# Rotary rows fetched by DMA within SBUF and copied to PSUM by ScalarE, in place of a TensorE product, beside three in-projections

## The reference

```python
def rope(x, pos):
    d = x.shape[-1]
    ...
    x1, x2 = xf[..., :d // 2], xf[..., d // 2:]
    return jnp.concatenate([x1 * cos - x2 * sin, x2 * cos + x1 * sin], axis=-1).astype(x.dtype)
```

## Time and profile before

| | |
|---|---|
| median of three runs | 3206.18 us (3196.72 to 3207.56) |
| profiled execution | 3206.65 us, span 3204.9 us |
| granted TensorE clock, mean | 0.969 of full speed |
| busy TensorE / VectorE / ScalarE / GpSimd | 3026.6 / 1619.9 / 1035.1 / 1096.7 us |
| layer 1's in-projection | about 993 to 1081 us |
| layer 2's | about 1706 to 1882 us |
| layer 3's | about 2438 to 2613 us |

### The profile page before, as it was taken

The page is one execution under the profiler, slowest core; times in us unless marked ns, Lnnn a source line. Parts: engine busy times, 40 slices in busy tenths (PEclk is TensorE's granted clock), DMA queues, the critical chain, the costliest instruction groups (busy, mean ns, idle before and its releaser), DMA issues.

```text
span 3204.9 us, 47400 instructions
## 1 busy us (share of the span) xinstructions
PE 3026.6 (94%) x16972; PEld 2445.0 (76%) x16972; DVE 1619.9 (51%) x2705; ACT 1035.1 (32%) x1842; POOL 1096.7 (34%) x634
## 2 busy tenths in 40 slices
PE   6998899999999898999998998999999999999997
PEld 4766688888877766889886766788877867688886
DVE  3466677753336574524236866442343367642423
ACT  4153421111224364322234334422223236532222
POOL 1262133323223313344442410344445311244443
PEclk8999999999999999999998998999999999999999
DMA  6202144433221002232321210323324100123322
GB/s 258 104 24 79 40 131 144 151 125 125 64 61 47 21 2 73 65 92 91 92 92 56 79 34 4 105 92 98 98 86 119 53 27 1 35 98 93 97 93 84
DMA packets 73202, 258.97 MB, mean 81 GB/s; under 512 B 9328, under 2 KB 11889, under 8 KB 70513
## 3 DMA queue, kind: packets, MB, share of 16 engines
q1 hardware_dynamic: 60256, 205.61, 20.4%
q10 hardware_dynamic: 12816, 51.65, 4.7%
HBM read 253.03 MB, written 2.10 MB: 80 GB/s over the span
## 4 chain that ended last, share of the span: by engine, by line
PE 85%; DVE 5%; issue 4%; ACT 2%; POOL 1%; ACTq 1%; DMA 1%; PEld 1%; POOLq 1%; SPq 1%; DVEq 0%; PEldq 0%
PE ps L852 59%; PE ps L818 7%; PE ps L2725 3%; PE ps L2739 2%; DVE ps L398 1%; PE ps L2893 1%; PE ps L2222 1%; PE ps L435 1%; PE ps L1123 1%; PE ps L2028 1%; PE ps L2955 1%; PE ps L2033 1%; ACT w_hi L638 1%; POOL w_lo L776 1%; PEld ps L852 1%
## 5 line engine op out<-in xcount | busy, mean ns | idle before, releaser
L776 POOL TENSOR_TENSOR w_lo<-w_raw,w_hi 128x1024 fp32r<-128x1024 f32 (+1 forms) x373 | 920.7, 2470 | 1752.9 <-ACT w_hi L638 1613.8
L638 ACT ACTIVATE w_hi<-w_raw 128x1024 fp32r<-128x1024 f32 (+1 forms) x373 | 386.2, 1038 | 1194.8 <-PE ps L852 984.8
L852 PE MATMUL ps<-h_hi,w_hi 128*128 128x258 f32 (+2 forms) x1824 | 327.4, 322 | 28.9 <-ACT w_hi L638 15.4
L852 PEld LDWEIGHTS ps<-h_hi,w_hi 128*128 128x128 f32 x1824 | 269.6, 191 | 64.4 <-ACT w_hi L638 17.3
L852 PE MATMUL ps<-h_lo,w_hi 128*128 128x258 f32 (+2 forms) x1824 | 317.0, 316 | 0.0
L852 PE MATMUL ps<-h_hi,w_lo 128*128 128x258 f32 (+2 forms) x1824 | 316.8, 316 | 0.0
L852 PEld LDWEIGHTS ps<-h_hi,w_lo 128*128 128x128 f32 x1824 | 267.8, 190 | 23.9
L852 PEld LDWEIGHTS ps<-h_lo,w_hi 128*128 128x128 f32 x1824 | 268.3, 190 | 23.3
L940 DVE CAST act_hi<-f_t 128x512 f32 (+1 forms) x88 | 167.5, 1903 | 12.5
L852 PE MATMUL ps<-hb_hi,w_hi 128*128 128x512 f32 x672 | 166.7, 390 | 1.8 <-issue 1.8
L852 PE MATMUL ps<-act_hi,w_hi 128*128 128x512 f32 (+1 forms) x660 | 153.4, 373 | 14.1 <-ACT w_hi L638 13.5
(11 more groups left out here) (357 smaller groups left out, 4940.5 us busy)
## 6 DMA issues: line engine op xcount, KB each, us to landing
w_raw<-in_ffn_in SPq DMA_DIRECT2D x176, 512.0 KB, 3.5
mod_row<-in_w_mod_rows ACTq DMA_DIRECT2D x64, 512.0 KB, 4.4
w_raw<-in_ffn_out SPq DMA_DIRECT2D x64, 512.0 KB, 3.5
w_raw<-in_ev_in SPq DMA_DIRECT2D x26, 512.0 KB, 3.5
w_raw<-in_ffn_out SPq DMA_DIRECT2D x32, 384.0 KB, 3.0
w_raw<-in_od_in SPq DMA_DIRECT2D x21, 512.0 KB, 3.5
mod_ring<-in_w_mod SPq DMA_DIRECT2D x8, 1024.0 KB, 14.3
wide_ring<-in_w_mod_wide ACTq DMA_DIRECT2D x8, 1024.0 KB, 5.0
```

What stands on the lines that cost most here:

```text
L638: act.activation(k.w_hi[:, s, 0:self.KT * P], k.w_raw[:, s, 0:self.KT * P], ACT.Copy).then_inc(k.sems["w_hi_ready"], 1)
L776: ins = pool.tensor_tensor(k.w_lo[:, s, 0:self.KT * P], k.w_raw[:, s, 0:self.KT * P], k.w_hi[:, s, 0:self.KT * P].bitcast(F32), ALU.subtract)
L852: ins = pe.matmul(k.ps[:, self.step * s + g, 0:t1 - t0], w[:, s, c * P:(c + 1) * P], h[:, c, t0:t1], start=(n == 0), stop=(n == len(parts) ...
```

## The change

- TensorE's product of line 1123 is gone for layers 1 to 3 (`tensor` does nothing in `RopeBeside`; layer 0 keeps its own). The minus sign that was in the matrix is now in the first half of each group of the sine table, and the matrix of layer 0 loses its sign likewise.
- SP, after issuing the load of slab m, waits until the tile of slab m - 4 is out and until the copy of the tile two before it has been made, and issues 128 / half transfers of half rows x 2 KB each within SBUF: `swapped` gets the tile with the halves of each group exchanged. `swapped` has two buffers. After the last slab SP does this for four more turns.
- ScalarE, at turn s + 3, waits for these transfers and for the bank (`rot_done`), and copies `swapped` into the bank.
- VectorE's steps of the rotation move one turn later (multiply and add at turn s + 2, low part at s + 3), ScalarE's high part too (s + 4). GpSimd's cosine product stays.
- What builds on the rotated tiles moves one turn later: the index scores, RELUs and sums, the rounds and the selection in layer 2; `FIRST` = 12 in layer 3.

```diff
+            if isinstance(self.beside, RopeBeside):
+                self.beside.sync(sp, m)
 
         self.slabs(sp, load)
+        if isinstance(self.beside, RopeBeside):
+            for m in range(self.M, self.M + RopeBeside.BEHIND):
+                self.beside.sync(sp, m)
...
+    BEHIND = 4
...
-    def tensor(self, pe, m):
-        n = self.at(m - 1)
+    def sync(self, sp, m):
+
+        n = self.at(m - self.BEHIND)
         if n is None:
             return
-        self.is_out(pe, m - 1)
-        if n >= len(self.BANKS):
-            pe.wait_ge(*self.count("rot_done", n - len(self.BANKS) + 1))
-        pe.matmul(self.bank(n), self.tiles[n].get("rot", self.rot), self.src(n), start=True, stop=True).then_inc(self.kit.sems["rot_mm"], 1)
+        self.is_out(sp, m - self.BEHIND)
+        if n >= 2:
+            sp.wait_ge(*self.count("rot_in_psum", n - 1))
+        h = self.tiles[n].get("half", self.half)
+        for p in range(0, P, h):
+            q = p + h if p // h % 2 == 0 else p - h
+            sp.dma_start(self.swapped[p:p + h, n % 2, :], self.src(n)[q:q + h, :]).then_inc(self.kit.sems[f"swapped{n % 2}"], 16)
+
+    def tensor(self, pe, m):
+        pass
...
     def vector(self, dve, chain, m):
         S = self.kit.sems
-        n = self.at(m - 2)
+        n = self.at(m - 3)
...
-        n = self.at(m - 1)
+        n = self.at(m - 2)
         if n is not None:
             tile = self.tiles[n]
-            dve.wait_ge(*self.count("rot_mm", n + 1))
+            dve.wait_ge(*self.count("rot_in_psum", n + 1))
...
     def scalar(self, act, chain, m):
+        n = self.at(m - 4)
+        if n is not None and "lo" in self.tiles[n]:
+            tile = self.tiles[n]
+            act.wait_ge(*self.count("rot_sum", n + 1))
+            if "plain" in tile:
+                act.activation(tile["plain"], self.bank(n), ACT.Copy)
+            if tile["hi"].shape[-1] > SEQ:
+                act.activation(tile["hi"][:, SEQ:], self.linear.tile(m - 4)[:, 0, SEQ:], ACT.Copy)
+            act.activation(tile["hi"][:, 0:SEQ], self.bank(n), ACT.Copy).then_inc(self.kit.sems["rot_hi"], 1)
         n = self.at(m - 3)
...
+        if n is not None:
+            act.wait_ge(self.kit.sems[f"swapped{n % 2}"], self.b_dma[n % 2] + 16 * sum(self.dmas[n % 2][:n // 2 + 1]))
+            if n >= len(self.BANKS):
+                act.wait_ge(*self.count("rot_done", n - len(self.BANKS) + 1))
+            act.activation(self.bank(n), self.swapped[:, n % 2, :], ACT.Copy).then_inc(self.kit.sems["rot_in_psum"], 1)
...
-    SCORES, TURNED, OUT, PAIRS, FIRST = 2, 3, 6, 8, 11
...
+    SCORES, TURNED, OUT, PAIRS, FIRST = 2, 3, 6, 8, 12
...
-            out[p, 0], out[p, 1] = np.cos(ang), np.sin(ang)
+            out[p, 0], out[p, 1] = np.cos(ang), np.sin(ang) * f(-1 if p % group < half else 1)
```

More of the change, by code:

```diff
@@ L1084, with __init__ @@
     BANKS = (4, 5, 6)
-    def __init__(self, kit, linear, rot, table, rot_c, tiles):
-        self.kit, self.linear, self.rot, self.table, self.rot_c = kit, linear, rot, table, rot_c
+    BEHIND = 4
+    def __init__(self, kit, linear, half, table, rot_c, swapped, tiles):
+        self.kit, self.linear, self.half, self.table, self.rot_c, self.swapped = kit, linear, half, table, rot_c, swapped
         self.tiles = tiles
         linear.attach(self)
-        self.b = {name: kit.reserve(name, len(tiles)) for name in ("rot_mm", "rot_cos", "rot_sum", "rot_done")}
+        self.b = {name: kit.reserve(name, len(tiles)) for name in ("rot_in_psum", "rot_cos", "rot_sum", "rot_done")}
         self.b["rot_hi"] = kit.reserve("rot_hi", sum("lo" in tile for tile in tiles))
+        self.b_dma, self.dmas = [], []
+        for e in range(2):
+            self.dmas.append([P // tile.get("half", half) for tile in tiles[e::2]])
+            self.b_dma.append(kit.dma_count(f"swapped{e}", sum(self.dmas[e])))
     def at(self, s):
@@ L1174, with __init__ @@
     AT = 6
-    def __init__(self, kit, linear, rot, table, rot_c, tiles, first_v, v_tok, keys):
-        super().__init__(kit, linear, rot, table, rot_c, tiles)
+    def __init__(self, kit, linear, half, table, rot_c, swapped, tiles, first_v, v_tok, keys):
+        super().__init__(kit, linear, half, table, rot_c, swapped, tiles)
         self.first_v, self.v_tok, self.keys = first_v, v_tok, keys
@@ L1238, with __init__ @@
     GATES, MAIN, SMALL = slice(0, 192), slice(192, 320), slice(320, 384)
-    SCORES, TURNED, OUT, PAIRS, FIRST = 2, 3, 6, 8, 11
-    def __init__(self, kit, linear, rot, table, rot_c, tiles, w1, w1_in, first_v, toks, q0):
-        super().__init__(kit, linear, rot, table, rot_c, tiles)
+    SCORES, TURNED, OUT, PAIRS, FIRST = 2, 3, 6, 8, 12
+    def __init__(self, kit, linear, half, table, rot_c, swapped, tiles, w1, w1_in, first_v, toks, q0):
+        super().__init__(kit, linear, half, table, rot_c, swapped, tiles)
         self.q0 = q0
@@ L1669, with __init__ @@
     PAIRS, ROUNDS, LATENT, NOPE, VALUES = 4 * QT, TOPK // 8, 6, 8, 22
-    def __init__(self, kit, linear, rot, table, rot_c, tiles, loaded, w_uk):
-        super().__init__(kit, linear, rot, table, rot_c, tiles)
+    def __init__(self, kit, linear, half, table, rot_c, swapped, tiles, loaded, w_uk):
+        super().__init__(kit, linear, half, table, rot_c, swapped, tiles)
         self.loaded, self.w_uk = loaded, w_uk
@@ L1747, in scalar @@
             act.dma_start(k.w_uk[:], self.w_uk).then_inc(S["uk_in"], 16)
-        if 6 <= m < 10:
-            for u in range((m - 6) * QT, (m - 5) * QT):
+        if 7 <= m < 11:
+            for u in range((m - 7) * QT, (m - 6) * QT):
                 out, n = self.pair(u)
@@ L1789, in vector @@
             dve.wait_ge(*self.count2("iw_in", 1))
-        if 4 <= m < 8:
-            self.add_scores(dve, chain, m - 4)
-        if m == 8:
+        if 5 <= m < 9:
+            self.add_scores(dve, chain, m - 5)
+        if m == 9:
             dve.wait_ge(*self.count2("idx_acc", self.PAIRS))
@@ L2850, in plan @@
                    [(0, 1, HD ** -0.5), (1, 2, 8 ** -0.5), (2, 7, 1.0), (7, 8, A_SCALE), (8, 18, 1.0), (18, 22, HD ** -0.5), (22, 26, 1.0)], norm=g.pre, tiles=EV_TILES, close=True)
[L2851 to L2852 removed]
+    small_rope = {"half": 16, "table": k.table[:, 1]}
+    LatentBeside(k, ev_in, 32, k.table[:, 0], k.rot_c2, k.swapped2,
                  [{"slab": s} for s in (0, 2, 3, 4, 5)] + [{"slab": s, **small_rope} for s in (7, 12, 13)]
@@ L3083, in rot @@
         for p in range(P):
-            if p % group < half:
-                m[p + half, p] = -1
-            else:
-                m[p - half, p] = 1
+            m[p + half if p % group < half else p - half, p] = 1
         return m
```

29 lines of the change are left out of this document (10 added, 19 removed).

## The result

The changed kernel took 3184.02 us (median of 6, 3182.56 to 3188.13) against 3205.78 us of the kernel before (median of 6): a ratio of 0.9935 with a 95% interval of 0.9925 to 0.9945. In a later series, beside three of the experiments, it took 3186.52 (median of 5) against 3204.43: 0.9948 (0.9935 to 0.9962). The gain is 18 to 22 us; 26.8 were forecast, and the time was forecast as 3180. The first trace has a span of 3184.7 us.

The account below looks back on a forecast made before the run. TensorE, busy for 94% of the span, was taken to bound the kernel. 35.8 us removed less 5.4 (index scores) and 3.6 (VectorE's lag and layer ends) gave 26.8 off 3206.18: 3179.4, say 3180; range 3168 to 3200.

Parts of the forecast that it names:

- Removed, 35.8 us: TensorE, layers 1 to 3: 40 rotations removed, 10 at 0.85 us and 30 at 0.91 us, 35.8 us in all.
- SyncE's period p: Layer 1 to 3 transfers: time per issue 0.43 us, 0.46 with the gap; a layer 1 turn is 0.36 + 8p = 4.0 us.
- the ring: Layer 1, weight split through GpSimd, SP, landing and copy to next split but one: 10.2 of 11.4 us, fits below p = 0.61.
- the queue: SP's turn in layer 1, 0.36 + 8p, binds when it exceeds TensorE's 5.7 us, at p = 0.67.
- rival 1: Layer 1: copies pace it mildly, at p = 0.97 a turn takes 8.1 us; 19 us back, 3199 us; chance 15%.
- 8 x excess: Layer 1: eight slabs each charged the SP turn's excess over 5.7 us, 8 x 2.4 = 19 us at p = 0.97.
- Rival 2: Layer 1: copies pace it fully, p from 1.1 us, and the kernel is slower, 3226 us at p = 1.26; chance 8%.
- (a) Index scores, 5.4 us: Layer 2's score groups: rotation worth 0.38 us there (1.6 lost), copies ahead of RELUs 1.8, late rows 2.0; bounds 1.6 and 10.
- (b) VectorE behind in layer 2, 0.8 us at the end: Layer 2's top-k rounds: DVE falls behind 0.52 us per slab, last selection ends some 0.8 us after today's next-stage start.
- (c) Ends, 1.4 + 1.4 us: Ends of layers 1 and 3: multiply and add ahead of V tile, 2 x 0.7 us; last compressed pair moved, 1.4 us.
- Layer 3, 11.3 us forecast: Layer 3's gain: removed work less the forecast's losses there, 11.3 us.

Follow-up runs that it names:

- 16 transfers: Changed kernel with each layer 1 tile fetched by sixteen transfers of 8 rows instead of eight of 16: 3231.91 us, ratio 1.0083 to the kernel before.
- the RELUs first: Changed kernel with ScalarE's RELUs of layer 2's index scores ahead of its copy of swapped rows: 3178.64 us, ratio 0.9920 to the kernel before.

## Why the forecast held, and where its terms were off

The sign, the size and the range were right (3180 forecast, 3184 and 3187 measured), and so was the shape: TensorE bound the kernel, the removed work counted almost in full in plain slabs, and what was lost was lost at the score groups and the ends. The terms:

- **Removed, 35.8 us.** Right. Free of the clock's part the three layers gained 7.2, 6.9 and 10.4 us, 24.5 together, against a forecast of 26.8 for just that. Slabs start 5.70 us apart in layer 1 and 5.44 in layer 2's plain ones, to the hundredth.
- **SyncE's period p, taken as 0.46 us: too low by a third and more.** It was 0.62 to 0.74 as a mean over eight, with the load 0.58. By the forecast's own test (the ring binds from 0.61, the queue from 0.67) layer 1 was over the limit, and rival 1 began there: loads 6.19 us apart against slabs of 5.70. It cost nothing because there is a lead at the start, 3.1 us by ScalarE's splits (one ready at 1004.35 for the slab at 1007.41), of which 0.3 was left; my sum of "8 x excess" charged every turn and left out that lead. That the error did not reach the time was luck: nothing in the forecast says that the layer ends before the lead does. The row I chose, the 64 KB constant with 0.43 us, was nearest in size, but its neighbours would have warned me: it is the last of 17 issues of line 271 that follow one another, eight of which took 0.43 us and the other nine 0.57 to 4.07, among them 2.11 for `rot_a`. The upper bound was too low as well: the other four copies of kc (line 1387) took up to 1.82 us. The copies of kc, which I put aside for their size, were the better kind, since size hardly counts. The Trainium skill's 0.95 us for 64 KB ("DMA: Bandwidth & Descriptors", Bandwidth) gave an estimated turn of 7.6 us: too long, but on the right side of 5.7, where my 4.0 was not. That is chance too, since the page's figure is the time of the DMA engines for a load from HBM, and not that of an issue.
- **Rival 2** is real as a mechanism, though not here: at 16 transfers the queue paced the layer and the kernel was slower than before (ratio 1.0083).
- **(a) Index scores, 5.4 us: 8.5 measured** (the forecast's 1.6 for a rotation's smaller worth there, and 6.9). The place and the cause were right: 5 to 6 us was forecast for the first group (7.30 measured) and under 4 for the others, and ScalarE waited 1.86 us for the rows where 2.0 was forecast. The measured groups sum to 19.9 us, 13.0 with the RELUs first. Of these 6.9 us, 4.2 are waiting, against 3.8 forecast. Missed were two things. ScalarE waited 0.52 us for rows in the fourth group as well, whose tile takes eight transfers instead of four (5.59 us). And a pause of 1.8 to 3.1 us in TensorE is not paid once: the clock fell around it, which made up the other 2.7 us (3.4 in the layer). In the second trace of the changed kernel it fell in the first group alone (7.79 us), and the fourth took 4.41.
- **(b) VectorE behind in layer 2, 0.8 us at the end.** VectorE fell behind as forecast, 5.99 us per slab where 5.96 was forecast, but the delay didn't wait for the end. ScalarE's high part waited for VectorE's sum (3.92 us), the copy of V rows stood behind it, and TensorE waited 1.73 us before a V transpose where it hadn't waited before. Right engine, wrong route.
- **(c) Ends, 1.4 + 1.4 us.** The first V wait of layer 1 grew from 2.77 to 4.11 us, 1.34. Layer 3 without the clock's part gained 10.4 us of the 12.7 removed there, so 2.3 were lost and not 1.4; where, no run shows.
- **Layer 3, 11.3 us forecast, 5.3 measured.** What failed is a term that the forecast doesn't have: it priced everything at a clock of 1.0 and never asked what the clock would do without the removed products. 5.1 of the missing 6.0 us are the clock's in this trace, and the second trace of the same kernel gave 3.4 of them back.

## What to carry to other kernels

Price a small transfer by the piece and by rows in which several stand in a row in the queue, and then count how many turns the lead covers: a queue slower than the loop is free for a while. When a step that waits for a DMA is put into an in-order engine, put it behind whatever TensorE waits for there, not ahead; here that order alone was worth 7 us of layer 2. And read the clock beside every pause of TensorE: with the pause of 3.1 us ahead of the scores went a fall that cost 1.7 us in one trace of the changed kernel and 3.4 in the other.

## What the runs showed of the hardware that I had not expected

- SyncE issues transfers within SBUF at 0.60 (64 KB), 0.62 and more (32 KB) and 0.67 us (16 KB) each when several follow one another. A single one takes 1.4 to 1.6 us now and then (three of the 80 in layer 1). The 512 KB weight load mostly takes 0.58 us between groups of eight, 0.44 between groups of sixteen, and 0.33 between groups of four.
- A 128x512 multiply on VectorE takes 0.69 us with one operand in PSUM, also when it begins inside GpSimd's weight split (14 of 40). With both in SBUF it takes 0.68 to 0.72 us, but one that begins inside GpSimd's weight split ends 0.55 us after the split does, and takes up to 2.9 us.
- TensorE's granted clock fell to 0.5 with no idle time at all, in runs of products of 124 columns and of one column, and by different amounts in executions of the same kernel (10.2 and 6.8 us in one layer).
